# State-space steps of a hybrid trunk: both scan pairs first in each group of four steps, convolution tiles over all sixteen

## The reference

```python
u, qkv, z, a_lg, b_lg, gate_a, gate_b = jnp.split(proj, split_at, axis=-1)
y_s5, s5r, s5i = s5_ssm(u, ...)                  # complex diagonal state-space scan over the tokens
y_s5 = jax.nn.gelu(y_s5)
qkv_c, conv_new = causal_conv(qkv, conv0, ...)   # 4 taps along the tokens, then silu
q, k, v = jnp.split(qkv_c, 3, axis=-1)           # l2 norms, then the gated delta rule
```

## Time and profile before

| | |
|---|---|
| median of 3 runs | 2065.47 us (2063.43 to 2067.73) |
| profiled execution | 2063.8 us |
| its span in the trace | 2062.0 us |
| PE busy | 2002.0 us, 97% |
| DVE busy | 1510.3 us, 73% |
| ACT busy | 1067.2 us, 52% |
| POOL busy | 154.7 us, 8% |

### The profile page before, as it was taken

The page is one execution under the profiler, slowest core; times in us unless marked ns, Lnnn a source line. Parts: engine busy times, 40 slices in busy tenths (PEclk is TensorE's granted clock), DMA queues, the critical chain, the costliest instruction groups (busy, mean ns, idle before and its releaser), DMA issues.

```text
span 2062.0 us, 30297 instructions
## 1 busy us (share of the span) xinstructions
PE 2002.0 (97%) x11446; PEld 1671.3 (81%) x11446; DVE 1510.3 (73%) x2181; ACT 1067.2 (52%) x1305; POOL 154.7 (8%) x247
## 2 busy tenths in 40 slices
PE   7999999999999999999999999999999999999996
PEld 3768887899998778888788788887888878788884
DVE  6894414555574975234799998999989899898986
ACT  2214111445432232111487776777778777787773
POOL 3540010000005330010000000000000000000000
PEclk9999999999999899999999999999999999999997
DMA  8575334555552454425399999999989999899992
GB/s 346 181 258 202 142 129 153 185 184 182 175 184 72 164 197 167 144 97 173 122 343 372 341 356 318 355 370 342 352 314 360 369 341 346 322 359 371 339 340 96
DMA packets 143051, 523.92 MB, mean 254 GB/s; under 512 B 16192, under 2 KB 16704, under 8 KB 142272
## 3 DMA queue, kind: packets, MB, share of 16 engines
q1 hardware_dynamic: 140544, 508.82, 68.9%
q10 hardware_dynamic: 1728, 7.90, 1.1%
q0 software_dynamic: 640, 5.35, 0.7%
HBM read 515.57 MB, written 6.43 MB: 253 GB/s over the span
## 4 chain that ended last, share of the span: by engine, by line
PE 84%; DVE 11%; POOL 2%; ACT 2%; issue 1%; DMA 1%; ACTq 0%; DVEq 0%
PE bank L919 26%; PE bank L274 16%; PE bank L945 15%; PE bank L778 12%; PE bank L442 4%; DVE wlo L2150 3%; DVE arena L1392 2%; PE bank L866 1%; PE bank L458 1%; PE bank L906 1%; DVE slab L1641 1%; ACT whi L1229 1%; PE bank L606 1%; PE bank L737 1%; PE bank L876 1%
## 5 line engine op out<-in xcount | busy, mean ns | idle before, releaser
L2150 DVE TENSOR_TENSOR wlo<-ring,whi 128x1024 fp32r<-128x1024 f32 x756 | 910.1, 1222 | 155.4 <-ACT whi L1229 149.8
L1229 ACT ACTIVATE whi<-ring 128x1024 fp32r<-128x1024 f32 x756 | 798.9, 1059 | 304.9 <-PE bank L919 151.7
L274 PE MATMUL bank<-hT,ring 128*128 128x264 f32 x1408 | 332.8, 396 | 6.0 <-issue 3.1
L274 PEld LDWEIGHTS bank<-hT,ring 128*128 128x128 f32 x1408 | 271.0, 195 | 59.7 <-issue 12.4
L919 PE MATMUL bank<-whi,gh 128*128 128x512 f32 x896 | 285.8, 400 | 3.9 <-DVE wlo L2150 3.0
L919 PE MATMUL bank<-whi,gl 128*128 128x512 f32 x896 | 279.5, 393 | 0.0
L919 PE MATMUL bank<-wlo,gh 128*128 128x512 f32 x896 | 278.7, 392 | 0.0
L919 PEld LDWEIGHTS bank<-wlo,gh 128*128 128x128 f32 x896 | 168.2, 188 | 39.1
L919 PEld LDWEIGHTS bank<-whi,gl 128*128 128x128 f32 x896 | 168.1, 188 | 37.9
L919 PEld LDWEIGHTS bank<-whi,gh 128*128 128x128 f32 x896 | 161.1, 188 | 37.9 <-DVE wlo L2150 6.7
L945 PE MATMUL bank<-whi,eh 128*128 128x512 f32 x448 | 142.3, 399 | 3.2 <-DVE wlo L2150 3.2
(11 more groups left out here) (387 smaller groups left out, 2414.4 us busy)
## 6 DMA issues: line engine op xcount, KB each, us to landing
ring<-in_w SPq DMA_DIRECT2D x964, 512.0 KB, 5.2
out_gdns<-arena POOLq DMA_DIRECT2D x2, 2048.0 KB, 7.8
arena<-in_gdn ACTq DMA_DIRECT2D x2, 1536.0 KB, 6.8
xT<-in_x ACTq DMA_DIRECT2D x1, 1056.0 KB, 9.0
out_y<-hT SPq DMA_DIRECT2D x4, 264.0 KB, 2.1
arena<-in_gdn ACTq DMA_DIRECT2D x2, 512.0 KB, 4.0
masks<-in_masks ACTq DMA_DIRECT2D x1, 512.0 KB, 11.1
cpk<-in_cpk SPq DMA_DIRECT2D x1, 512.0 KB, 5.3
```

Of the source, the lines that this page charges most:

```text
L274: ins = pe.matmul(out, w, rhs, start=start, stop=stop)
L1229: act.activation(whi[:, m % SPL, :], ring[:, r, :], ACT.Copy).then_inc(sem("hi_done"), 1)
L2150: v.tensor_tensor(wlo[:, m % SPL, :], ring[:, (low.base + m) % RING, :], whi[:, m % SPL, :].bitcast(F32), ALU.subtract).then_inc(sem("lo_d ...
```

## The change

In every group of four steps DVE before ran: pair, convolution tile, pair, tile, tile, tile, for three groups, and in the fourth pair, `conv_samples`, pair. Now every one of the four groups runs: pair, pair, tile, tile, tile. The twelve tiles are spread over four groups instead of three, and `conv_samples` stands in the last step instead of step 12. The lists of PE, ACT, POOL and SP keep their order.

```diff
                 for j in range(S5_STEPS):
-                    if j % 4 < 2:
-                        s5_pair(l, 2 * (j // 4) + j % 4)
+                    if j % 4 == 0:
+                        for b in range(2):
+                            s5_pair(l, j // 2 + b)
                     if j == 1:
                         s5_step_out(l)
-                    if j < QT:
-                        conv_tile(l, j)
-                    elif j == QT:
+                    if j % 4:
+                        conv_tile(l, 3 * (j // 4) + j % 4 - 1)
+                    if j == S5_STEPS - 1:
                         conv_samples(l)
```

## The result

The changed kernel took 2049.03 us (median of 4 runs, 2048.42 to 2051.11), the kernel before beside it 2064.93 (4 runs): a ratio of 0.9933, with a 95% interval of 0.9919 to 0.9947, which is 10.9 to 16.7 us less. A second comparison, with more runs, gave 0.9941 (0.9919 to 0.9963), 7.6 to 16.7 us. The 11.1 us of the sum lie in both intervals, and 2049 in the range. The profiled execution took 2051.11 us (2063.8 before), its span is 2049.3.

The account below looks back on a forecast made before the run. PE, busy 97% of the span, was taken as the bound, waiting for banks that DVE gives back. Layer 0's 5.71 us and layer 1's 5.35 made 11.1 less: 2052.7 for the profiled execution, 2054 as median, range 2048 to 2061.

Parts of the forecast that it names:

- the sum: Both layers: 5.71 us won in layer 0 and 5.35 in layer 1, together 11.1 us less.
- Pair 3's bank: Loop, second group: bank back at 104.7 and near 704.5, so PE's stalls of 3.21 and 2.24 us go.
- The clock: Behind pair 3's stall: the slow stretch goes, 1.58 us in layer 0; layer 1 has 3.11 with its stall.
- The rival that it falls all the same: Clock falls behind the same stretch, or elsewhere once PE stands differently: 6.4 us less, 2059; chance 0.13.
- The second pair's loss: Second pair beside POOL's rotation: sum waits for the second step, first scan for the third; 1.7 us lost.
- The rival that blocked all five instructions one by one: Each SBUF instruction of a second pair waits for a rotation step, about 5.5 us lost per pair: 2073; chance 0.05.
- Pair 1's bank: Layer 0, first group: bank back at 84.23, wanted by PE at 86.71.
- The 0.92 us go: Layer 0: PE's 0.92 us stall at a projection, waiting for pair 1's bank, disappears.
- the prediction's own signs: Right: line 1613 holds PE up nowhere, projections take 7.4 us; wrong: granted clock near 0.5 in the loop, among others.
- The later groups: Pairs 4 to 7 move ahead of tiles at no cost; pair 5's bank is free 7 us early.
- the new wait of the rival: PE, 5.5 us earlier to weights, banks and square, waits anew: 0 to 3 us left, 2062 to 2066; chance 0.12.
- The end of the loop: `conv_done` at about 153.8 and 759.7, costing nothing with 6.9 and 4.5 us to spare before the token sums.

Follow-up runs that it names:

- its tile put back: The changed kernel with one convolution tile again between pairs 2 and 3: 2061.78 us, ratio 0.9994 to the kernel before.
- the filled stall: The changed kernel with a tile again between pairs 2 and 3, plus useless PE products ahead of those waiting for pair 3's bank: 2056.99 us, ratio 0.9971.
- the first group put back: The changed kernel with tile 0 again between pairs 0 and 1: 2049.03 us, ratio 0.9945 to the kernel before.
- the second group alone: The kernel before with only pair 3 moved directly behind pair 2: 2056.86 us, ratio 0.9977.
- the kernel that takes it off PE's path: The changed kernel with PE's input products of pairs 2 and 3 behind the projections of their step: 2044.76 us, ratio 0.9907 to the kernel before.
- the wrong one alone: The kernel before with only pair 1 moved directly behind pair 0, tile 0 behind both: 2065.55 us, ratio 1.0015.

## Why the prediction was right, point by point

*Pair 3's bank: right, in place and size.* It came back at 104.57, forecast 104.7, and at 703.53 + 0.69 = 704.2 in layer 1, forecast 704.5. From the start of the wait to the end of the projections, layer 0 took 3.21 + 2.76 + 8.59 us before and takes 2.37 + 7.39 now, 4.80 less; the sum had 3.21 + 1.58 = 4.79. Layer 1 has lost 2.24 + 3.73 + 9.15 - 2.38 - 7.39 = 5.35, and the sum had 5.35. With its tile put back the gain is gone; alone it gives about half. In the second trace of the changed kernel PE still stands 1.34 us there in layer 1, so this place is only just covered.

*The clock: right behind pair 3.* The rival that it falls all the same behind that stretch fell in both layers. Its other half, that the clock falls elsewhere once PE stands differently, came true at pair 1's bank, below. That the idle time made it fall was an assumption in the prediction; the filled stall shows it.

*The second pair's loss: right.* 1.78 - 0.69 + 2.15 - 1.37 = 1.87 us, taken 1.7. The sum waited for the second rotation step and one scan for the third, as forecast, though the sum took 1.78 us and not about 1.4. In pair 1 of layer 0 the order was another and the loss nearly the same: the sum began at 84.06, just ahead of GpSimd's second step at 84.08, and kept its 0.69 us, the step took 1.79 instead of 1.28, and the four scans took 3.17. The rival that blocked all five instructions one by one is out: three scans ran free, since the rotation was over. The traces agree with the Trainium skill's rule in "SBUF — State Buffer", section "Who interferes with whom", for scans too: of the 64 scans in the trace after the median took 398 ns, the longest 1375.

*Pair 1's bank: the step that failed in the trace.* "The 0.92 us go" took PE's time of before, 86.71, as given. The bank came back at 83.33 + 0.69 = 84.02, forecast 84.23. But in the profiled execution after, PE was some 4 us earlier by then, because the clock did not fall ahead of the loop as it had before, and so it waited 0.78 and 1.07 us, with 10.26 - 7.39 = 2.87 us of slow clock behind. By the prediction's own signs this step was wrong: it named line 1613 holding PE up nowhere as a sign of being right, and a granted clock near 0.5 in the loop as one of being wrong, and the clock was 0.53 there. What the 0.92 is worth on the median no run shows: with the first group put back the time is the same. What was missing is that this place stays the next bound whenever PE comes early; the kernel that takes it off PE's path has a median 4.3 us lower, but its trace does not show the reason.

*The later groups: right as a cost, wrong as a side matter.* They cost nothing that the traces show: PE waits for none of their banks. But their moves were counted at nothing won either, and the second group alone shows that without them the wait goes on to pair 5, 1.95 us and a slow stretch.

*Weights.* No term was given to them. Twice in layer 0 the conditioning products (16 rows) take longer than the usual 1.92 us, 0.4 and 0.6 more:

```profile
126.12 2.28 PE L458 MATMUL bank<-ring,cT 128*32 128x512 f32 x16
139.57 1.92 PE L458 MATMUL bank<-ring,cT 128*32 128x512 f32 x16
148.74 2.51 PE L458 MATMUL bank<-ring,cT 128*32 128x512 f32 x16
```

In both, PE's weight loads (PEld) wait for a slot to land:

```profile
127.35 0.14 PEld L458 LDWEIGHTS bank<-ring,cT 128*32 128x32 f32 x4 [0.22 <-DMA ring<-in_w]
...
150.20 0.14 PEld L458 LDWEIGHTS bank<-ring,cT 128*32 128x32 f32 x4 [0.45 <-DMA ring<-in_w]
```

It is the new wait of the rival, at a tenth of its size.

*The end of the loop: right.* `conv_done` came at 153.98 (forecast 153.8), and the token sums started at 167.10 and 763.44 (near 166 and 764). In layer 1 `conv_done` came at 753.2 (forecast 759.7, which did not count that layer 1's loop begins earlier: in the profiled pair by 6.1 us).

*The total.* The profiled pair differs by 12.7 us, the medians by 15.9 and 13.6, the sum by 11.1. In the profiled pair layer 0 gave less than its sum: pair 3's input products start 110.80 - 106.87 = 3.93 us earlier (the sum had 4.13), 1.59 came behind them, the weights took 0.95 back, and the token sums start 4.58 us earlier instead of 5.71. That the 3.93 is so near 4.13 is luck: PE wanted the first of the banks at 80.59 - 0.78 = 79.81 instead of 84.26, 4.45 us earlier, which no step of the prediction gives, and lost 0.78 + 1.07 + 2.87 = 4.72 at the first two pairs, where it had lost 0.92 before. Layer 1 gave its 5.35; 1.5 us more came between the two loops and 1.3 behind the second. So the total came out right with one term of it wrong. The difference of the medians to the sum is within the intervals and can't be given to a cause: what the clock does ahead of the loop differs from execution to execution, by some 4 us.

## What to carry to other kernels

Where PSUM banks go round, look for every place at which the next reader is as late as the one that you mend, and mend them together: one alone moved a part of the wait to the next, and the wrong one alone made the kernel no faster. Price a stall of PE with the slow stretch behind it, which was worth 1.6 to 3.1 us beside waits of 3.2 and 2.2. Ask of a wait that is only just covered what happens when PE comes 4 us earlier.

## What the runs showed of the hardware

- Useless products in PE's idle time made a kernel 4.8 us faster; the granted clock behind them stayed at 1.00 instead of 0.50.
- In the traces told of here, each of the ten waits of PE in the loop that lasted 1.95 us or more had a slow stretch behind it. Shorter ones had it in part: at pair 1's bank in layer 0 six waits of 0.75 to 1.07 us had it and two of 0.60 and 0.92 had not; at other places 0.55, 1.32 and 1.34 us had not (waits of 0.68 to 0.78 at pair 0's bank, just ahead of pair 1's, are not counted). The six are of executions whose clock had not fallen just ahead of the loop, the two of executions where it had. Length alone does not decide: ahead of layer 1's loop PE waits 1.94 to 1.99 us for ACT in all thirteen traces, and in three of them only is there a slow stretch behind. What tells these apart stays open.
- Just ahead of layer 0's loop the clock fell in six of the thirteen traces and not in the others, of programs that are the same up to there: to 0.50 at 54.6 and 61.4 us in the trace of before, not there in that of after. It moves PE by some 4 us, and with it what the next wait costs.
- A sum with both inputs in SBUF took 1.78 us behind the start of a GpSimd step instead of 0.69, a scan up to 1.375 instead of 0.398; where the sum began first, the step took 1.79 instead of 1.28; line 1613, with one input in PSUM, 691 to 692 ns in all 16 cases.
